# Output projection, LayerNorm, modulation and router logits by token tile, with an adaLN wave moved behind the routing

## What is computed

```python
sh1, sc1, g1, sh2, sc2, g2 = adaln(cond, w_ada[i], b_ada[i])   # silu(cond) @ w_ada + b_ada, in six
out = attention(...) @ w_o                                     # (tokens, 1024) @ (1024, 1024)
x = layer_norm(ALPHA * x + g1 * out, ln_g[i, 0], ln_b[i, 0])
h = x * (1 + sc2) + sh2                                        # modulation
g_logits = h @ w_rg + b_rg                                     # 4 groups
e_logits = h @ w_re + b_re                                     # 32 experts
# top group, its two best experts; every expert: (silu(h @ w_gate) * (h @ w_up)) @ w_down
```

## Time and profile before

| | us |
|---|---|
| median of 3 runs | 1601.62 (1598.58 to 1602.39) |
| the profiled execution | 1598.8, its span 1597.0 |
| PE busy | 1110.6 (70%) |
| DVE busy | 404.2 (25%) |
| ACT busy | 170.1 (11%) |
| POOL busy | 210.9 (13%) |
| mean DMA rate | 249 GB/s |
| chain that ended last | PE 44%, DMA 37%, DVE 10% |

### The profile page before, as it was taken

The page is one execution under the profiler, slowest core; times in us unless marked ns, Lnnn a source line. Parts: engine busy times, 40 slices in busy tenths (PEclk is TensorE's granted clock), DMA queues, the critical chain, the costliest instruction groups (busy, mean ns, idle before and its releaser), DMA issues.

```text
span 1597.0 us, 25857 instructions
## 1 busy us (share of the span) xinstructions
PE 1110.6 (70%) x9606; PEld 587.1 (37%) x9607; DVE 404.2 (25%) x906; ACT 170.1 (11%) x460; POOL 210.9 (13%) x359
## 2 busy tenths in 40 slices
PE   3899977888448767865219998999426577877720
PEld 1333444424224433432114445774323234443310
DVE  0011177354201111110091112322741011111116
ACT  0110143001000000000000003440000000000000
POOL 0000000000112322331100000000002122322220
PEclk9899967896679988997659998899559689998975
DMA  8776300287699999999914423010039999699830
GB/s 330 267 263 251 94 25 1 103 311 311 267 423 388 424 423 426 381 425 424 422 56 141 123 79 105 1 51 3 40 133 409 424 426 424 246 423 384 359 150 40
DMA packets 84327, 398.26 MB, mean 249 GB/s; under 512 B 14656, under 2 KB 14944, under 8 KB 56640
## 3 DMA queue, kind: packets, MB, share of 16 engines
q1 hardware_dynamic: 61136, 341.91, 52.9%
q0 software_dynamic: 16240, 53.09, 9.1%
q10 hardware_dynamic: 6912, 2.76, 0.6%
HBM read 381.12 MB, written 16.72 MB: 249 GB/s over the span
## 4 chain that ended last, share of the span: by engine, by line
PE 44%; DMA 37%; DVE 10%; issue 3%; ACT 2%; DVEq 1%; SPq 1%; POOL 0%; ACTq 0%; POOLq 0%
PE ps L684 21%; DMA ring<-in_w_down_dram 20%; DMA ring<-in_w_up_dram 10%; PE ps L893 6%; PE ps L911 4%; DMA ring<-in_w_ada_dram 2%; PE ps L802 2%; DMA qkv<-ybuf 2%; PE ps L660 2%; PE ps L769 2%; DMA x<-in_x_sample_dram 1%; PE ps L840 1%; PE ps L787 1%; PE ps L776 1%; DMA ring<-in_w_gate_dram 1%
## 5 line engine op out<-in xcount | busy, mean ns | idle before, releaser
L893 PE MATMUL ps<-ring,xs 128*32 128x256 f32 x4736 | 313.9, 420 | 142.6 <-DMA ring<-in_w_up_dram 89.1
L893 PEld LDWEIGHTS ps<-ring,xs 128*32 128x32 f32 x4736 | 175.8, 119 | 273.1 <-issue 200.1
L684 PE MATMUL ps<-ring,hT 128*128 128x512 f32 x576 | 255.4, 604 | 5.3 <-ACT hT L536 4.2
L911 PE MATMUL ps<-ring,hm 128*32 128x256 f32 x2368 | 150.9, 393 | 36.7 <-ACT hm L630 27.1
L684 PEld LDWEIGHTS ps<-ring,hT 128*128 128x128 f32 x576 | 110.8, 194 | 148.8 <-issue 141.0
L1294 DVE TENSOR_TENSOR hp<-sg,ps 128x128 f32<-128x128 f32 x74 | 21.3, 288 | 330.1 <-ACT sg L627 330.1
L911 PEld LDWEIGHTS ps<-ring,hm 128*32 128x32 f32 x2368 | 69.4, 112 | 95.9 <-ACT hm L630 41.6
L1302 DVE COPY yo<-ps 128x256 f32<-128x256 f32 x74 | 31.4, 425 | 240.3 <-DMA ybuf<-yo,idy 161.4
L684 PE MATMUL ps<-ring,qT 128*128 128x512 f32 x192 | 84.9, 605 | 2.3 <-ACT qT L559 2.3
L627 ACT ACTIVATE sg<-ps 128x128 f32<-128x128 f32 x74 | 20.5, 277 | 616.0 <-PE ps L893 616.0
L451 POOL DMA_INDIRECT xg<-xmod,idx x78 | 77.3, 991 | 61.7 <-POOL idx L448 60.9
(11 more groups left out here) (194 smaller groups left out, 833.2 us busy)
## 6 DMA issues: line engine op xcount, KB each, us to landing
ring<-in_w_gate_dram SPq DMA_DIRECT2D x82, 1024.0 KB, 15.0
ring<-in_w_up_dram SPq DMA_DIRECT2D x82, 1024.0 KB, 15.2
ring<-in_w_down_dram SPq DMA_DIRECT2D x82, 1024.0 KB, 15.2
ring<-in_w_ada_dram SPq DMA_DIRECT2D x48, 1024.0 KB, 8.9
ring<-in_w_qkv_a_dram SPq DMA_DIRECT2D x12, 1024.0 KB, 5.1
ring<-in_w_qkv_b_dram SPq DMA_DIRECT2D x12, 1024.0 KB, 11.8
modb<-mdram POOLq DMA_DIRECT2D x12, 512.0 KB, 8.8
qkv<-ybuf POOLq DMA_DIRECT2D x2, 3072.0 KB, 15.6
```

The source lines that it names most:

```text
L684: ins = mm(ps[:, 2 * t + hf, :], lhs[:, k, t * P:(t + 1) * P], raw[:, slot, kk * D + hf * 512:kk * D + (hf + 1) * 512], start=(k == 0), st ...
L893: ins = mm(ps[j * BLK:(j + 1) * BLK, 1, 0:W].rearrange("p (a n) -> p a n", a=2), xs[:, k, :], w[:, :, at:at + FW], start=(k == 0), stop=(k ...
L911: ins = mm(ps[j * BLK:(j + 1) * BLK, 5, 0:WD], hm[:, 2 * c + q, :], ring[:, slot + GU + c, q * D + j * WD:q * D + (j + 1) * WD], start=(c ...
```

## The change

W_o comes in four chunks of 1 MB (`WO_N`). `wo_tile(t)` projects one tile over all four chunks; the chunks are held until tile 2 has used them, and tiles 0 and 1 raise a new semaphore, `wo_done`. The order on PE becomes: tile 0, tile 1, turn of tile 0, tile 2, turn of tile 1, logits of tiles 0 and 1, in layer 0 wave 3, turn of tile 2, logits of tile 2, in layer 0 wave 4, the routing matmuls, and in layer 0 wave 5 behind the last of them (L872). ACT follows that order; `take_ada(5)` stands ahead of its first expert block. `layer_norm_rows` on DVE does a tile from residual to scaling (`scale_rows`, the former L1020 and L1021) before the next, with a reciprocal root of its own. POOL stores the modulated rows tile by tile. The first expert load waits for all chunks of the ring (`MOE0[l] + RING`) instead of slot by slot. Waves 4 and 5 change banks. Since there are two chunks less ahead of layer 1's QKV, its prefetches start with slot 4. The second LayerNorm (stage 1) keeps its order.

The diff, cut (a line of "..." leaves out unchanged lines, the indentation is shortened, and the part that takes stage 0 out of `layer_norm` is left out):

```diff
-WO_K = (2, 2, 1, 1, 1, 1)
+WO_N = 4
...
-ADA1 = WO0[0] + RING
+ADA1 = WO0[0] + WO_N
...
-MOE0 = [QKV_B, WO0[1] + RING]
+MOE0 = [QKV_B, WO0[1] + WO_N]
...
-ADA_BANK = (6, 6, 7, 7, 6, 0)
+ADA_BANK = (6, 6, 7, 7, 0, 6)
...
-                sp.wait_ge(*taken(0, cidx, freed))
+                sp.wait_ge(*taken(0, n % RING, freed))
...
-        k = 0
-        for cidx, nk in enumerate(WO_K):
-            n = WO0[l] + cidx
+        for c in range(WO_N):
+            n = WO0[l] + c
...
-            sp.dma_start(raw[:, n % RING, 0:nk * D].rearrange("p (k n) -> p k n", k=nk),
-                         wo[:, k:k + nk, :]).then_inc(st_land[n % RING], 16)
-            k += nk
+            sp.dma_start(raw[:, n % RING, :].rearrange("p (k n) -> p k n", k=2),
+                         wo[:, 2 * c:2 * c + 2, :]).then_inc(st_land[n % RING], 16)
...
-            sp.wait_ge(xmod_w[l], 16)
+            sp.wait_ge(xmod_w[l], 16 * NT)
...
-                    sp.wait_ge(st_free, MOE0[l] + s + 1)
+                    sp.wait_ge(st_free, MOE0[l] + RING)
...
-        pool.wait_ge(xm_rdy[l], NT)
-        pool.dma_start(xmod.rearrange("(t p) d -> p t d", p=P), qkv[:, :, 0:D]).then_inc(xmod_w[l], 16)
+        for t in range(NT):
+            pool.wait_ge(xm_rdy[l], t + 1)
+            pool.dma_start(xmod[t * P:(t + 1) * P, :], qkv[:, t, 0:D]).then_inc(xmod_w[l], 16)
...
-        pool.wait_ge(xmod_w[l], 16)
+        pool.wait_ge(xmod_w[l], 16 * NT)
...
-    def take_transposed(dst, done, ready):
-        for t in range(NT):
+    def take_transposed(dst, done, ready, tiles=range(NT)):
+        for t in tiles:
...
+        take_transposed(hT, xT_ps[l], xT_rdy[l], range(2))
...
+        take_transposed(hT, xT_ps[l], xT_rdy[l], range(2, NT))
+        if l == 0:
...
-        take_transposed(hT, xT_ps[l], xT_rdy[l])
-        if l == 0:
-            take_ada(5)
...
+        if l == 0:
+            take_ada(5)
...
-    def transpose_tiles(src, ready, done, rows=by_stride):
-        for t in range(NT):
+    def transpose_tiles(src, ready, done, rows=by_stride, tiles=range(NT)):
+        for t in tiles:
...
-        k = 0
-        for cidx, nk in enumerate(WO_K):
-            n = WO0[l] + cidx
-            wait_chunk(pe, n)
-            project(oT, nk, k, n % RING, False, None)
-            k += nk
-        if l == 0:
-            for i in (3, 4):
-                for k in range(KD):
-                    ada_wave(i, k)
-        transpose_tiles(lambda t: qkv[:, t, 0:D], xm_rdy[l], xT_ps[l], by_run)
-        pe.wait_ge(xT_rdy[l], NT)
-        if l == 0:
-            pe.wait_ge(ld_wr, 16 * LAYERS * (2 * G * G + 2))
-            pe.wait_ge(mblk_ev, 5)
+        def wo_tile(t):
+            for c in range(WO_N):
+                n = WO0[l] + c
+                if t == 0:
+                    wait_chunk(pe, n)
+                for kk in range(2):
+                    k = 2 * c + kk
+                    for hf in range(2):
+                        ins = mm(ps[:, 2 * t + hf, :], oT[:, k, t * P:(t + 1) * P],
+                                 raw[:, n % RING, kk * D + hf * 512:kk * D + (hf + 1) * 512],
+                                 start=(k == 0), stop=(k == KD - 1))
+                if t == NT - 1:
+                    ins.then_inc(st_free, 1)
+                elif c == WO_N - 1:
+                    ins.then_inc(wo_done[l], 1)
+        def turn_x(t):
+            transpose_tiles(lambda t: qkv[:, t, 0:D], xm_rdy[l], xT_ps[l], by_run, (t,))
...
-        for t in range(NT):
+        def logits(t):
+            pe.wait_ge(xT_rdy[l], t + 1)
...
-        ins.then_inc(rt_pe[l], 1)
-        if l == 0:
+            return ins
+        wo_tile(0)
+        wo_tile(1)
+        turn_x(0)
+        wo_tile(2)
+        if l == 0:
+            pe.wait_ge(ld_wr, 16 * LAYERS * (2 * G * G + 2))
+        turn_x(1)
+        logits(0)
+        logits(1)
+        if l == 0:
...
-                ada_wave(5, k)
+                ada_wave(3, k)
+        turn_x(2)
+        logits(2).then_inc(rt_pe[l], 1)
+        if l == 0:
+            for k in range(KD):
+                ada_wave(4, k)
...
+        if l == 0:
+            for k in range(KD):
+                ada_wave(5, k)
...
+    def layer_norm_rows(l):
+        dve.wait_ge(lnb_ld, 64 * (2 * l + 1))
+        for t in range(NT):
+            sc = 0 if t == 0 else 2
+            if t < NT - 1:
+                dve.wait_ge(wo_done[l], t + 1)
+            else:
+                dve.wait_ge(st_free, RING + MOE0[l] - (3 * KD if l == 0 else 0))
+            chain(v.tensor_tensor(t1[:, :], tile_ps(t), lnb[:, 0 if t == 0 else 1, :], ALU.mult))
+            chain(v.scalar_tensor_tensor(x[:, t, :], x[:, t, :], ALPHA, t1[:, :], ALU.mult, ALU.add))
+            for i in range(2):
+                v.bn_stats(st[:, i, :], x[:, t, i * 512:(i + 1) * 512])
+            dve.drain()
+            chain(v.bn_aggr(mv[:, t, :], st[:, :, :].rearrange("p a b -> p (a b)")))
+            chain(v.tensor_scalar(var[:, 0:1], mv[:, t, 1:2], EPS, None, ALU.add))
+            rsqrt(rstd[:, 0:1], var[:, 0:1], newt[:, 0:1])
+            chain(v.tensor_scalar(x[:, t, :], x[:, t, :], mv[:, t, 0:1], rstd[:, 0:1], ALU.subtract, ALU.mult))
+            chain(v.tensor_tensor(t1[:, :], x[:, t, :], modb[:, sc, :], ALU.mult))
+            v.tensor_tensor(qkv[:, t, 0:D].rearrange("p (j b r) -> p j r b", j=G, b=KD),
+                            t1[:, :].rearrange("p (j r b) -> p j r b", j=G, b=KD),
+                            modb[:, sc + 1, :].rearrange("p (j r b) -> p j r b", j=G, b=KD),
+                            ALU.add).then_inc(xm_rdy[l], 1)
+            dve.drain()
+            scale_rows(t)
+        dve.sem_inc(mod_used, 1)
+    def scale_rows(t):
+        chain(v.tensor_tensor(x[:, t, :], x[:, t, :], lnb[:, 2, :], ALU.mult))
+        chain(v.tensor_tensor(x[:, t, :], x[:, t, :], lnb[:, 3, :], ALU.add))
...
-        dve.wait_ge(st_free, RING + WO0[l] + RING)
-        layer_norm(l, 0, tile_ps, xm_rdy[l])
+        layer_norm_rows(l)
```

More of the change, by code:

```diff
@@ L218, in backbone_kernel @@
         qkv_done, qkv_ev = sem2("qkv_done"), sem2("qkv_ev")
+        wo_done = sem2("wo_done")
         roped = sem("roped")
@@ L1003, in layer_norm @@
                         sc = 0 if t == 0 else 2
-                        if stage == 0:
-                            chain(v.tensor_tensor(t1[:, :], x[:, t, :], modb[:, sc, :], ALU.mult))
-                            v.tensor_tensor(qkv[:, t, 0:D].rearrange("p (j b r) -> p j r b", j=G, b=KD),
-                                            t1[:, :].rearrange("p (j r b) -> p j r b", j=G, b=KD),
-                                            modb[:, sc + 1, :].rearrange("p (j r b) -> p j r b", j=G, b=KD),
-                                            ALU.add).then_inc(ready, 1)
-                        else:
-                            chain(v.tensor_tensor(qkv[:, t, 0:D], x[:, t, :], modb[:, sc, :], ALU.mult))
-                            v.tensor_tensor(qkv[:, t, 0:D], qkv[:, t, 0:D], modb[:, sc + 1, :], ALU.add).then_inc(ready, 1)
-                        if stage == 0:
-                            dve.drain()
+                        chain(v.tensor_tensor(qkv[:, t, 0:D], x[:, t, :], modb[:, sc, :], ALU.mult))
+                        v.tensor_tensor(qkv[:, t, 0:D], qkv[:, t, 0:D], modb[:, sc + 1, :], ALU.add).then_inc(ready, 1)
                 if ready is not None:
@@ L1019, in layer_norm @@
                 for t in range(NT):
-                    chain(v.tensor_tensor(x[:, t, :], x[:, t, :], lnb[:, 2, :], ALU.mult))
-                    chain(v.tensor_tensor(x[:, t, :], x[:, t, :], lnb[:, 3, :], ALU.add))
-                    if stage == 1:
-                        dve.sem_inc(x_rdy[l], 1)
+                    scale_rows(t)
+                    dve.sem_inc(x_rdy[l], 1)
             for l in range(LAYERS):
```

## The result

| | before | after |
|---|---|---|
| median of the timed runs, us | 1602.01 (1598.58 to 1603.83, 4 runs) | 1572.57 (1569.01 to 1579.06, 4 runs) |
| the profiled execution, us | 1598.8, span 1597.0 | 1571.02, span 1569.2 |
| predicted, us | | 1567 (1558 to 1577) |

The ratio is 0.983, with a 95% interval of 0.98 to 0.986: by it the change takes 27 us off (29.4 between the medians), where the prediction had 32.1.

The account below looks back on a forecast made before the run. Bound by PE, DVE and ACT working one after the other (42.1 us in layer 1), with full DMA engines in layer 0. 23.2 + 8.9 = 32.1 us off 1598.8 gives 1566.7, forecast 1567, range 1558 to 1577.

Parts of the forecast that it names:

- Layer 1: Layer 1, projection to logits: only tile 2's LayerNorm exposed, DVE on the logits at 1134.9 instead of 1158.15, 23.2 us less.
- What would show it: Signs: in layer 1 DVE waits on PE three times, logits about 60 us in; wrong if DVE's tile outlasts PE's.
- Layer 0: Layer 0, projection to first expert load: counting 19.8 us earlier, part put back by wave 5, 8.9 us less.
- SP's load goes out at 390.8 + 12.1 = 402.9: Layer 0's first expert load: token table at 390.8, wave 5 behind it, load at 402.9 instead of 411.85.
- the price of a wave at full clock: Layer 0, wave 3: 0.89 us a wave, bias and first wave done at 345.6, wave 3 at 353.9.
- Wave 5: Layer 0, behind the last routing matmul: 11.9 us put back, 10.1 at full clock, 15.5 at half.
- The sum: Whole kernel: 23.2 + 8.9 = 32.1 us off the profiled 1598.8, so 1566.7.
- What I had costed at nothing: Four W_o chunks, three stores, new PSUM banks, reordered prefetches of layer 1's QKV weights: 0 us, prefetches +-2.
- Layer 0 gives nothing: Layer 0: waves 4 and 5 end 9 us later, experts start when they did; 1575.6 us, chance 0.10.
- Full clock in the tail: Layer 1's turn and last logits, layer 0's first logits and wave 5 faster: 7 us more, 1560, chance 0.08.
- The projection loses its clock: Both layers' projections: turns drop the clock to half for tiles 1 and 2, 27.7 us each; 1622, chance 0.03.
- No overlap: LayerNorm held to the projection's end, three separate roots add 5.7 us, little left: 1598, chance 0.02.

Follow-up runs that it names:

- Experiment 2: Changed kernel, but LayerNorm waits for the whole projection and goes tile by tile from there: 1631.09 us, ratio 1.0176 to the kernel before.
- layer 0 alone: Changed kernel with the new order of PE, ACT and DVE in layer 0 only, layer 1 in the old: 1591.51 us, ratio 0.9933 to before.

## Why the prediction came out

**Layer 1: right.** The term was 23.2 us, the stage gave 22.9. The steps held one by one: 14.2 and 13.8 us a tile on DVE against 13.85; a one-column root at the price of the three-column one (from 1087.69 to 1090.84, 3.15 against 2.87, of which one gap of 0.42); only tile 2 exposed; the last turn at 1.98 and its logits in 3.64 at a clock of 0.50. From projection to logits 60.3 us, the number that "What would show it" had. Two of the signs in "What would show it" were too strict: DVE waited for PE ahead of tiles 0 and 2 only, and its first tile took 0.3 longer than PE's, which PE's turn of tile 0 (0.87) covered. Experiment 2 shows that it is the overlap that pays, and the stage came to 85.75 to 85.99 us in all nine profiles that have this order with its overlap in layer 1.

**Layer 0: mechanism right, the term mis-sized.** The step that failed is the sum that ended with "SP's load goes out at 390.8 + 12.1 = 402.9", 110.3 us behind the projection's start: it had wave 3 and wave 5's last chunk too cheap. In the profile it is 115.7. Counted from that start:

| event, us behind the projection's start | predicted | after |
|---|---|---|
| logits of tiles 0 and 1 done | 51.2 | 48.9 |
| last chunk of wave 3 landed | 60.4 | 61.6 |
| wave 3 done | 61.3 | 63.3 |
| DVE starts on the logits | 66.9 | 68.4 |
| counting | 82.6 | 84.9 |
| last routing matmul done | 98.2 | 101.0 |
| first expert load | 110.3 | 115.7 |

- The first logits came 2.3 us early, since PE was still at full clock (3.68 us for two tiles instead of 5.8). That gained nothing, as wave 3 then ran its bias and first waves at half clock, 1.8 instead of 0.9 each; its eighth chunk went out at 348.04 and landed 7.29 us later. Price of both: 2.0 at the end of wave 3. So the price of a wave at full clock, taken from the earlier trace rows, was wrong for this execution, but not for all. In the profile of layer 0 alone, with the same instructions behind the same logits, the bias took 0.99 and two waves 1.90 (the row below).
- Wave 4's stream kept that delay (2.3 at the counting), and the routing took 0.5 more than its 15.6.
- **Wave 5**: 14.5 us of work and waiting instead of 11.9, inside the bounds of 10.1 and 15.5. The seventh chunk landed as predicted, 8.6 us behind the last routing matmul. The eighth landed 3.9 behind it instead of 2.47, 6.98 from its issue, and its wave ran at half clock, 1.98 instead of 0.9. The trace of the kernel before had this very pair of loads in its wave 5 (issued 1.7 us apart, the second landing after 6.48 us), and would have been the better row for it than the earlier trace rows.

The row of the profile of layer 0 alone, whose order there is that of the kernel after:

```profile
340.00:344.00 4.00, 4.00 (x39) 1.87 (x42) 2.94 (x16) 0.00 (x0) 0.00 (x0) 1.00 0.48 203
```

There DVE starts on the logits after 64.5 us instead of 68.4, and the first load goes out after 111.3, near the 110.3 of the prediction, though by errors that cancel: the counting starts 1.8 early and the way from it to the load takes 30.6 instead of 27.7. Of the eight profiles that have wave 3 right behind the logits of tiles 0 and 1 with the overlap, two have it at full clock and six at half. What decides it, no run here shows.

In this execution layer 0 gave 3.5 us instead of 8.9. Others did better: with the new order the stage took 115.7, 112.8 and 111.3 us, with the old one 119.2, 116.7, 119.3 and 117.6. The means lie 4.9 apart, and the timed gain of layer 0 alone, 0.5 to 0.9%, is 8 to 14 us. So 8.9 was too much for the stage of most profiles, but the timed runs don't exclude it; the few microseconds between stage and time stay open.

**The sum.** 1566.7 was predicted and the profiled execution took 1571.0. The 4.3 between them are 5.5 of layer 0, 0.3 of layer 1 and 1.1 of a later start of the projection, less 2.25 in QKV and attention of layer 1 and 0.2 in the other stages. I put the 2.25 down to no edit. A kernel with the new order (wave 5 moved) took 234.1 us there as well, and the mean granted clock of that stretch goes with its length: 0.95 in these two profiles of 234.1 and 234.2 us, 0.96 to 0.97 in the seven of 230.5 to 232.3, 0.92 to 0.93 in the four of 239.0 to 240.6. No run isolates it. Against the medians the prediction is 5.6 low: the profile of before lay 3.2 under its median of 1602.01, that of after 1.6 under its own, which the range had allowed for.

**What I had costed at nothing** stayed at nothing where it could be read. The experts' stage is 376.2 against 376.8 with the first gather earlier and the prefetches in another order, and three stores of modulated rows are on no chain. The first expert load asking for all slots at once costs nothing that the scatter would show: with wave 5 out of the way (moved to layer 1, or ahead of the counting) it goes out 17.4 and 16.0 us behind the counting, in the old form 16.8 and 16.0 (395.02 to 411.85 in the earlier trace rows, and the second profile).

**The rivals.** (1) *Layer 0 gives nothing* was half true of this execution, by its mechanism (slow clock in both waves), though not to its size. (2) *Full clock in the tail* came true for the logits of layer 0, 3.68 us for two tiles instead of 5.8 and 1.98 for tile 2 instead of 2.9; layer 1's last logits stayed at 0.50 in all thirteen profiles, and wave 5 began at half clock. The rule that sustained activity releases the clock, on the page "TensorE: Matmul & The Clock Gate" of the Trainium skill, Part 1, describes the projection (1.00 over 56 us). It doesn't tell the clock of the logits and waves: there the clock stays at or falls to 0.50 with PE busy all the time in most profiles, while two have 1.00 through the first steps of the same wave 3. (3) *The projection loses its clock* didn't happen: 27.73 us for 64 matmuls and 13.75 for 32, with a turn of 0.87 between them. (4) *No overlap* is refuted for the change, and experiment 2 shows its price: not 1598 but 1631. The prediction counted the roots and forgot that each tile's scaling now stands ahead of the next tile's release (with the roots 4.3 us in layer 1). Above all it forgot that in layer 0 wave 3 waits behind the late logits, and waves 4 and 5 behind it (24.5 us).

## What to carry to other kernels

When three stages alternate on different engines over the same tiles, compare their times per tile first: here 13.9 us on PE met 14.0 on DVE, and all but the last tile's work disappeared. Then look at what stands on the same engine between a released tile and its consumer. When a stream has more chunks than its ring has slots (here eight and six), the last ones can only be issued once the first are used up: 7.0 to 9.6 us for the last chunk of each wave stand on the chain of the kernel after. So use up the first chunks early, in a gap of the engine, which also gives their slots back, and the late ones where another engine sets the pace. Look too at what stands behind such a load in the issuing engine's own queue; where the work isn't due, move it to a stage that waits for something else. Last, cut the span at the same events in both profiles before explaining a median: part of a difference may lie in a stage that the change doesn't touch.

## What I had not expected of the hardware

- The end of layer 1's attention runs at a granted clock of 1.00 in some executions and at 0.57 and 0.50 in others, in the same kernel: 6.4 us between the two profiles of the kernel before, more than the 3.5 that layer 0's stage gives in the profiled execution.
- A 1 MB load into a queue that carried only the one issued 1.7 us before it took 6.98 us from issue to landing (7.08 in a second profile), where the median of W_o's was 4.9. POOL had issued a gather 0.8 us before it; in the kernel before, where no gather is out yet, such a second load took 6.48. So most of the extra is the pair, and what the gather adds is not isolated.
- PE's busy share doesn't tell its clock here. It was busy 10.00 of 10.00 us with routing matmuls and waves at a mean clock of 0.60, and at 1.00 in 7 us with 5.04 busy in attention. Wave 3 behind the logits, the same instructions each time, began at 1.00 in two profiles and at 0.50 in six.
